# Three fp32r terms for the spatial unit's two projections, and parameter operations behind the first modulation

## What is computed

```python
z = jax.nn.gelu(hn @ c_w_in[j], approximate=False)     # 1024 -> 2048
u, vv = jnp.split(z, 2, axis=-1)
vv = layer_norm_2(vv, c_ln_g[j], c_ln_b[j])
h = h + spatial_gating(u, vv, c_w_s[j], c_b_s[j]) @ c_w_out[j]
h = h + moe_swiglu(rms_norm_2(h, ln_ffn[i]), ...)      # top 2 of 8 experts
```

## Time and profile before

| | us |
|---|---|
| median of 3 runs | 2120.82 (2120.63 to 2123.67) |
| the profiled execution | 2116.54 |
| its span, first to last instruction | 2114.8 |
| TensorE busy | 2023.5 (96%) |
| DVE busy | 1354.8 (64%) |
| ACT busy | 923.1 (44%) |

### The profile page before, as it was taken

The page is one execution under the profiler, slowest core; times in us unless marked ns, Lnnn a source line. Parts: engine busy times, 40 slices in busy tenths (PEclk is TensorE's granted clock), DMA queues, the critical chain, the costliest instruction groups (busy, mean ns, idle before and its releaser), DMA issues. The chain is left out here.

```text
span 2114.8 us, 28776 instructions
## 1 busy us (share of the span) xinstructions
PE 2023.5 (96%) x12095; PEld 1805.3 (85%) x12095; DVE 1354.8 (64%) x1671; ACT 923.1 (44%) x1066; POOL 71.5 (3%) x109
## 2 busy tenths in 40 slices
PE   4998999999999999999999989999999999999998
PEld 3876888787878877899998889999999999898976
DVE  6687897352464134666532269787878787878862
ACT  2511111212125102343432357676767676666654
POOL 2000000000000010100120000000000000000000
PEclk8998999999999999999999999999999999999999
DMA  9745221335143242255763259898989999899980
GB/s 319 262 122 172 66 81 61 120 135 185 40 159 119 81 161 100 63 191 186 192 233 133 83 199 367 313 356 323 356 322 335 346 330 346 328 352 331 348 316 21
DMA packets 225852, 452.22 MB, mean 214 GB/s; under 512 B 6944, under 2 KB 91176, under 8 KB 225720
## 3 DMA queue, kind: packets, MB, share of 16 engines
q1 hardware_dynamic: 222400, 445.44, 60.1%
q0 software_dynamic: 1632, 4.75, 0.8%
q10 hardware_dynamic: 1688, 0.15, 0.1%
HBM read 448.21 MB, written 2.10 MB: 213 GB/s over the span
## 5 line engine op out<-in xcount | busy, mean ns | idle before, releaser
L1752 DVE TENSOR_TENSOR ring_r<-ring,his_r 128x2816 fp32r<-128x2816 f32 (+1 forms) x192 | 587.1, 3086 | 59.8 <-ACT his_r L1360 59.6
L1360 ACT ACTIVATE his_r<-ring 128x2816 fp32r<-128x2816 f32 (+1 forms) x192 | 491.2, 2561 | 198.0 <-DMA ring<-in_moe_w_dram 184.6
L1046 PE MATMUL bank<-his_r,hg_r 128*128 128x352 f32 x2048 | 355.5, 325 | 0.8 <-ACT hg_r L1382 0.8
L1046 PEld LDWEIGHTS bank<-his_r,hg_r 128*128 128x128 f32 x2048 | 332.9, 188 | 2.0 <-issue 0.9
L2220 PE MATMUL bank<-hT,ring 128*128 128x256 f32 x912 | 218.0, 396 | 3.2 <-ACT hT L2542 1.8
L2220 PEld LDWEIGHTS bank<-hT,ring 128*128 128x128 f32 x912 | 177.4, 198 | 32.5 <-issue 7.0
L1046 PE MATMUL bank<-ring_r,hg_r 128*128 128x352 f32 x1024 | 186.1, 324 | 0.0
L2002 PE MATMUL bank<-arena,ring 128*128 128x256 f32 x800 | 178.2, 380 | 1.8 <-ACT cw L1302 0.7
L2002 PEld LDWEIGHTS bank<-arena,ring 128*128 128x128 f32 x800 | 151.3, 190 | 24.4 <-issue 1.3
L1046 PEld LDWEIGHTS bank<-ring_r,hg_r 128*128 128x128 f32 x1024 | 169.2, 188 | 0.0
L2002 PE MATMUL bank<-hT,ring 128*128 128x256 f32 x624 | 142.9, 387 | 5.0 <-ACT hT L2542 3.4
(11 more groups left out here) (495 smaller groups left out, 2529.7 us busy)
## 6 DMA issues: line engine op xcount, KB each, us to landing
ring<-in_moe_w_dram SPq DMA_DIRECT2D x128, 1408.0 KB, 8.3
ring<-in_moe_w_dram SPq DMA_DIRECT2D x48, 1536.0 KB, 8.8
ring<-in_even_w_in_dram SPq DMA_DIRECT2D x28, 1024.0 KB, 6.0
ring<-in_ffn_w_dram SPq DMA_DIRECT2D x22, 1024.0 KB, 5.4
ring<-in_ada_w_dram SPq DMA_DIRECT2D x20, 1024.0 KB, 9.4
ring<-in_odd_w_in_dram SPq DMA_DIRECT2D x9, 2048.0 KB, 7.7
ring<-in_moe_w_dram SPq DMA_DIRECT2D x16, 1024.0 KB, 6.5
ring<-in_a_w_in_dram SPq DMA_DIRECT2D x6, 2048.0 KB, 7.9
```

Of the source, the lines that this page charges most:

```text
L1046: ins = mm(bank[first + m][:, 0:WC], x[:, KT // 2 * late + k, :], w[:, k, WC * m:WC * m + WC], start=(not late and k == 0 and s == "hg_hi" ...
L1360: A(moe_hi(n), moe_w(n), ACT.Copy).then_inc(sem("moe_hi"), 1)
L1752: V.tensor_tensor(moe_lo(n), moe_w(n), moe_hi(n).bitcast(F32), ALU.subtract).then_inc(sem("moe_lo"), 1)
```

## The change

Tiles of `cin` and `cout` are computed in three fp32r terms. H2 becomes a pair: h2_r[0], the rounded value written by ACT, and h2_r[1], the remainder, by DVE (`rest`). CU gets its rounded copy from ACT and its remainder from DVE (`cu_lo`), a quarter at a time. The weights are split in 12 units u of two tiles: ACT casts (`c_cast`) into one of three buffers, DVE writes the remainder into the ring (`c_lo`). Casts 0 to 2 and remainders 0, 1 lie beside `pg0`, the others beside `cin` and `cout`. The heads (`c_first`) take hi and lo for both tiles over k, then the remainder of x. Second, three operations on AUX at the start of the kernel, with the wait for the parameters, are moved behind ada(3, 0) and the wait for the first norm.

```diff
--- before.py
+++ after.py
@@ -127,6 +127,9 @@
         fa_hi_r = sb_r("fa_hi_r", 12288, FT, T)
         fa_lo_r = sb_r("fa_lo_r", 17920, FT, T)
         f2_r = [sb_r(f"f2_r{n}", off, FT, P) for n, off in enumerate((25088, 0, 2816))]
+        cb_r = [sb_r(f"cb_r{n}", off, KT, T)[:, :, :] for n, off in enumerate((2048, 15360, 25088))]
+        h2_r = [sb_r("h2_hi_r", 13312, KT, T)[:, :, :], sb_r("h2_lo_r", 19456, KT, T)[:, :, :]]
+        cu_r = [sb_r("cu_hi_r", 21504, KT, T)[:, :, :], sb_r("cu_lo_r", 4096, KT, T)[:, :, :]]
         at_lo_r = sb_r("at_lo_r", 9984, FT, SLOTS)
         arena = sb("arena", [P, ARENA])
 
@@ -498,6 +501,22 @@
 
             return ffn_r[:, phases["f13"]["place"][j]["slot"]].rearrange("p (k n) -> p k n", k=KT)
 
+        C_HI = [cb_r[u % 3] for u in range(8)] + [cb_r[2 * (u % 2)] for u in range(4)]
+        C_FREE = {3: 0, 4: 1, 5: 2, 6: 3, 7: 4, 8: 6, 9: 5, 10: 8, 11: 9}
+
+        def c_half(u, flat=ring_flat):
+
+            name, v = ("cin", u) if u < 8 else ("cout", u - 8)
+            return view(phases[name], v // 2, flat)[:, :, T * (v % 2):T * (v % 2) + T]
+
+        def hi_made(u):
+
+            return u + 1 if u < 10 else u + 5
+
+        def c_done(u):
+
+            return phases["cin"]["t0"] + 2 * u + 2
+
         BCH_AT = [0, 2, 3, 5, 6, 8, 9, 11, 12]
         CONV_AT = {3: (0,), 4: (1,), 5: (2,), 6: (3,)}
         CGATE_AT = {7: (0, 1), 8: (2, 3)}
@@ -955,7 +974,45 @@
                     spatial_turn(2)
                     spatial_turn(3)
 
-            pe_gemm("cin", lambda k: H2[:, k, :], [], ready=xg_waits(5), lead=2, mid=lambda: norm_rest(5), prev="pg0", between=beside_cin)
+            def c_terms(q, x, bk, after):
+
+                u, m = q // 2, q % 2
+                hi, lo = C_HI[u], c_half(u, ring_r_flat)
+                for w, y in ((hi, x[0]), (hi, x[1]), (lo, x[0])):
+                    if w is lo:
+                        pe.wait_ge(sem("c_lo"), u + 1)
+                    for k in range(KT):
+                        ins = mm(bk[:, 0:T], w[:, k, m * P:m * P + P], y[:, k, :], start=(w is hi and y is x[0] and k == 0),
+                                 stop=(w is lo and k == KT - 1))
+                ins.then_inc(acc_ready, 1)
+                after(q % 16)
+
+            def c_first(u, x, ready, mid, last):
+
+                hi, lo = C_HI[u], c_half(u, ring_r_flat)
+                pe.wait_ge(sem("c_hi"), u + 1)
+                pe.wait_ge(sem("c_lo"), u + 1)
+                for k in range(KT):
+                    pe.wait_ge(*ready(k))
+                    for w in (hi, lo):
+                        for m in range(2):
+                            mm(bank[m][:, 0:T], w[:, k, m * P:m * P + P], x[0][:, k, :], start=(k == 0 and w is hi), stop=False)
+                mid()
+                for m in range(2):
+                    for k in range(KT):
+                        pe.wait_ge(*last(k))
+                        ins = mm(bank[m][:, 0:T], hi[:, k, m * P:m * P + P], x[1][:, k, :], start=False, stop=(k == KT - 1))
+                    ins.then_inc(acc_ready, 1)
+
+            for q in range(2):
+                pe.wait_ge(*took("pg0", 5 + q))
+            c_first(0, h2_r, xg_waits(5), lambda: norm_rest(5), lambda k: (sem("c_rest"), k + 1))
+            beside_cin(0)
+            beside_cin(1)
+            for q in range(2, 16):
+                pe.wait_ge(*(took("pg0", 5 + q) if q < 4 else took("cin", q - 3)))
+                pe.wait_ge(sem("c_hi"), q // 2 + 1)
+                c_terms(q, h2_r, bank[q % 4], beside_cin)
             pe.wait_ge(sem("toks_taken"), TK_V + 4)
             pe.wait_ge(sem("pool_made"), MADE["spatial"])
             for g in range(8):
@@ -987,8 +1044,13 @@
                     route(q - 4)
 
             pe.wait_ge(*took("cin", 16))
-            pe_gemm("cout", lambda k: CU[:, k, :], [], ready=lambda k: (sem("spatial_taken"), k // 2 + 1), lead=2, banks=2,
-                    parts=(range(0, 2), range(2, 4), range(4, 6), range(6, 8)), between=beside_cout)
+            c_first(8, cu_r, lambda k: (sem("c_hi"), 10 + k // 2 + 1), lambda: None, lambda k: (sem("c_rest"), KT + k // 2 + 1))
+            beside_cout(0)
+            beside_cout(1)
+            for q in range(2, 8):
+                pe.wait_ge(*took("cout", q - 1))
+                pe.wait_ge(sem("c_hi"), hi_made(8 + q // 2))
+                c_terms(16 + q, cu_r, bank[q % 2], beside_cout)
             norm_rest(6, 4)
             for ct in range(4, KT):
                 route(ct)
@@ -1316,12 +1378,21 @@
                 act.wait_ge(*took(f"pg{i}", q + 1))
                 A(PG[:, q, :], PG[:, q, :], ACT.Sigmoid).then_inc(sem("activated"), 1)
 
+            def c_cast(u):
+                name, v = ("cin", u) if u < 8 else ("cout", u - 8)
+                wait_chunk(act, name, v // 2, 0)
+                if u in C_FREE:
+                    act.wait_ge(acc_ready, c_done(C_FREE[u]))
+                A(C_HI[u], c_half(u), ACT.Copy).then_inc(sem("c_hi"), 1)
+
             for q in range(KT + 1):
+                if q in (1, 3, 5):
+                    c_cast(q // 2)
                 if q < KT:
                     gate(0, q)
                 if q >= 1:
                     act.wait_ge(sem("embedded"), q)
-                    A(H2[:, q - 1, :], xT[:, q - 1, :], ACT.Identity, scale=col("mix1", q - 1)).then_inc(sem("xg_ready"), 1)
+                    A(h2_r[0][:, q - 1, :], xT[:, q - 1, :], ACT.Identity, scale=col("mix1", q - 1)).then_inc(sem("xg_ready"), 1)
                     square(5, q - 1)
             root(5)
             def spatial_taken(b):
@@ -1332,6 +1403,11 @@
                 act.wait_ge(*took("cin", q + 1))
                 v = CU[:, q - KT, :] if q >= KT else CVV[:, q, :]
                 A(v, v, ACT.Gelu).then_inc(sem("activated"), 1)
+                if q % 2 == 1 and q < 10:
+                    c_cast(q // 2 + 3)
+                elif q == 13:
+                    c_cast(8)
+                    c_cast(9)
                 if q == 2:
                     for b in range(2):
                         act.wait_ge(sem("toks_ready"), TK_W + b + 1)
@@ -1351,6 +1427,9 @@
                     spatial_taken(1)
             spatial_taken(2)
             spatial_taken(3)
+            for b in range(4):
+                act.wait_ge(sem("spatial_taken"), b + 1)
+                A(cu_r[0][:, 2 * b:2 * b + 2, :], CU[:, 2 * b:2 * b + 2, :], ACT.Copy).then_inc(sem("c_hi"), 1)
 
             def hi(n):
 
@@ -1364,6 +1443,8 @@
                     hi(0)
                     hi(1)
                 act.wait_ge(*took("cout", q + 1))
+                if q in (1, 3):
+                    c_cast(10 + q // 2)
                 A(hT[:, q, :], xT[:, q, :], ACT.Identity, scale=col("ffn1", q)).then_inc(sem("xg_ready"), 1)
                 square(6, q)
             root(6)
@@ -1699,6 +1780,10 @@
                 step(V.tensor_tensor(FX[:, q % 2, :], bank[q % 4][:, 0:T], nr[:, :], ALU.mult))
                 V.tensor_tensor(xT[:, q, :], FX[:, q % 2, :], xT[:, q, :], ALU.add).then_inc(acc_taken["dve"], 1)
 
+            def c_lo(u):
+                dve.wait_ge(sem("c_hi"), hi_made(u))
+                V.tensor_tensor(c_half(u, ring_r_flat), c_half(u), C_HI[u].bitcast(F32), ALU.subtract).then_inc(sem("c_lo"), 1)
+
             def ple(i, nrm):
 
                 dve.wait_ge(sem("norm_rooted"), nrm + 1)
@@ -1706,14 +1791,30 @@
                 if i:
                     dve.wait_ge(*took("pp1", 8))
 
+                def rest(q):
+                    if i == 0:
+                        dve.wait_ge(sem("xg_ready"), KT * XN[5] + q + 1)
+                        V.scalar_tensor_tensor(h2_r[1][:, q, :], xT[:, q, :], col("mix1", q), h2_r[0][:, q, :].bitcast(F32), ALU.mult, ALU.subtract)\
+                            .then_inc(sem("c_rest"), 1)
+
                 def add(q):
                     dve.wait_ge(sem("activated"), (KT + 16) * i + q + 1)
                     step(V.tensor_tensor(PG[:, q, :], PG[:, q, :], (PP, PP1)[i][:, q, :], ALU.mult))
                     V.tensor_tensor(xT[:, q, :], xT[:, q, :], PG[:, q, :], ALU.add).then_inc(sem("embedded"), 1)
 
+                def beside(q):
+                    if q >= 1:
+                        add(q - 1)
+                    if q >= 2:
+                        rest(q - 2)
+                    if i == 0 and q in (3, 6):
+                        c_lo(q // 3 - 1)
+
                 take_gemm(dve, f"pg{i}", lambda q, lin, b: V.tensor_tensor(PG[:, q, :], b, RPG, ALU.mult), banks=(4, 2)[i],
-                          between=lambda q: add(q - 1) if q else None)
+                          between=beside)
                 add(KT - 1)
+                rest(KT - 2)
+                rest(KT - 1)
 
             ple(0, 4)
 
@@ -1721,6 +1822,10 @@
             step(V.reciprocal(RIN, nr[:, :]))
 
             def beside_cin(q):
+                if q % 2 == 0 and q < 12:
+                    c_lo(q // 2 + 2)
+                elif q >= 14:
+                    c_lo(q - 6)
```

(18 more changed lines are left out.)

## The result

| | median us | lowest to highest | profiled execution | its span |
|---|---|---|---|---|
| before | 2122.16 | 2120.63 to 2123.67 | 2116.54 | 2114.8 |
| after | 2110.84 | 2108.59 to 2111.79 | 2110.74 | 2109.0 |

After stands to before as 0.9943, with a 95% interval of 0.993 to 0.9956; of 2122 us that is 12.1 less, between 9.3 and 14.9. The medians themselves differ by 11.3. The forecast was -9.3 and 2111.5 us.

The account below looks back on a forecast made before the run. TensorE, almost without idle time, was taken as the bound in the projections and experts. Tiles -11.8, hand-over losses 0.1, 0.05, 1.25 and 1.2 gave -9.2; with -0.1 for the parameter operations, -9.3 from 2120.8: 2111.5 us, range 2106 to 2117.

Parts of the forecast that it names:

- The tile: In `cin` and `cout`, a tile of 24 matmuls takes 2.86 us, 0.59 less; 11.8 us over the 20 tiles outside the heads.
- Head of `cin`: Start of `cin`: c_lo(1) on DVE delays an eviction; TensorE idle 0.6 and 0.7 us; head gives back its 1.2 and 0.1.
- Layer norm and v: Tile 12 to the spatial matmuls: casts 8 and 9 on ACT delay the copies; 1.1 us gained of 2.36, 1.25 lost.
- Head of `cout`: After the spatial matmuls start: TensorE waits for CU's last two quarters; the head's own gain goes and 1.2 us more.
- The cover: Steady part of `cin`: per two tiles ACT and DVE need about 3.1 us, against TensorE's 2 x (2.86 + 0.43): covered.
- The squares: Layer norm's squares in `cin`: with cast 7 and remainder 7 around them, ACT arrives just when tile 10 ends; 0.05 us lost.
- Routing chain: Between `cout` and the experts: left as it is by the change and moved earlier as a block.
- that rival: Experts bound by the weight stream: their end does not move and the time stays at 2120.8 us; chance 0.06.
- the rival that ended slower: Gaps before the spatial matmuls and in `cout`'s head lower the clock for tiles 2 to 7: +4.3, 2125.1 us; chance 0.06.
- Parameter operations: At the kernel's start: moved, ada(2, 0) still waits for TensorE's group 0 sum; -0.1 us, between 0.1 more and 0.3 less.
- First z matmul: Behind the start's modulation: a shift of its start by more than 0.5 us would show the forecast wrong.
- The reference of the sum: Whole kernel: -9.3 us taken from the median of 2120.8, giving 2111.5; 2107.2 for an execution like the profiled one.

Follow-up runs that it names:

- The mended kernel: Changed kernel with cast 9 moved behind the layer norm's root on ACT and CU's four remainders behind all four products on DVE: 2109.42 us, ratio 0.9941.
- two kernels with a shifted balance: Changed kernel with an added DVE pass ahead of each of 12 weight remainders: 2128.94 us; changed kernel without the third term in 20 tiles: 2102.95 us.
- the kernel with the third accumulator: Changed kernel with a separate accumulator for column group 2, so ada(2, 0) doesn't wait for TensorE's sum of group 0: 2108.08 us, ratio 0.9933.

## Why the forecast held, step by step

From pg0 to the experts, by the distances of the two TensorE timelines:

| stretch | before | after | difference | forecast |
|---|---|---|---|---|
| pg0 to the end of pg0 | 28.05 | 27.87 | -0.18 | 0 |
| head of `cin`, to tile 2 | 8.22 | 8.49 | +0.27 | +0.1 |
| tiles 2 to 11 | 41.44 | 35.34 | -6.10 | -5.85 |
| tile 12 to the spatial matmuls | 16.79 | 15.26 | -1.53 | -1.1 |
| spatial matmuls to tile 2 of `cout` | 10.58 | 11.59 | +1.01 | +1.2 |
| tile 2 to the end of `cout` | 26.12 | 22.50 | -3.62 | -3.54 |
| routing chain | 20.73 | 21.34 | +0.61 | 0 |
| sum | | | -9.54 | -9.2 |

Outside the routing chain these distances repeat to 0.02 us in the other profiles with the same stage, two of the old one and three of the new. Without that chain the change is worth 10.15 us, 0.95 more than forecast, most of it in the tiles and before the spatial matmuls.

- **The tile.** 2.86 us forecast, 2.85 measured; 3.29 with the sum, 3.28 measured. The rule of the Trainium skill ("TensorE: Matmul & The Clock Gate", Part 3, The mechanism) by which such loads would stand bare isn't borne out: by the estimate from it a tile took some 5.4 us.
- **Head of `cin`.** Both waits came, from the releasers named: 0.23 (0.6 forecast) and 0.66 (0.7).
- **Layer norm and v.** Two waits, 0.83 and 0.69; tile 12 to the spatial matmuls 15.26 where I had 15.7. The mended kernel shows that cast 9 made the first of them, 0.69 us of the distance.
- **Head of `cout`.** Two waits of 0.72, both on ACT's casts; S + 11.59 where I had S + 11.75. The mended kernel shows that the order of DVE's remainders cost 1.15 of it.
- **The cover.** It held in the outcome, but the forecast's reason was short. It set 3.1 us on ACT and 3.1 on DVE side by side against 6.58, as if 3.5 were free; they stand in series, a round takes 4.92, and 1.64 are free.
- **The squares.** 0.05 us was right here. The two kernels with a shifted balance lost 5.80 and 4.06 us at exactly this place.
- **Routing chain.** The 0.61 us are not the change's: the gathering matmuls take 5.74 us in the profile of before, 6.34 in that of after, and 6.40 and 6.37 in the two other kernels that have the old stage.
- **Experts.** The distance to the end is 873.8 before and 873.7 after: nothing of the gain is lost to the weight stream, so that rival is out.
- **The clock.** 1.00 through both heads, so the rival that ended slower didn't happen. That its mechanism exists is seen in the two kernels with waits of 4 to 6 us. The Trainium skill ("TensorE: Matmul & The Clock Gate", Part 1) says that the array is throttled by default and that activity releases it; the traces agree, with 3.78 us for 8 sums behind the longest wait and 1.89 for the next 8, one tile later in the same kernel.
- **Parameter operations.** Releaser and mechanism as forecast, the sign was not: -0.1 forecast, with at most 0.1 more as the bad end; +0.19 measured. The slip is in the forecast's own sum. With the stall ending at 25.5 instead of 25.37 and the 0.23 us paid later on the same engine, what stands behind comes 0.13 us later and not 0.1 earlier.
- **First z matmul.** I had called a shift of over 0.5 us a sign of an error. It came, 2.5 us: 2.32 up to the sum for column group 0, by the late rise of the clock, and 0.19 by the move. What failed is the bound itself: I took it from one execution of before, and the start of the kernel has two forms.
- **The reference of the sum.** The stage and the move together say -9.4 against the profile of before and -10.0 against the two others with the old stage; the medians say -11.3, and the half without the move says 2111.08 at a ratio of 0.9954, or -9.8. The 1.3 to 1.9 us between lie within the interval, and well within what the untouched code scatters (below). That 2111.5 came within 0.7 us of 2110.84 is in part luck: the difference was forecast 2.0 us too small and the reference 1.3 too low.

## What to carry to other kernels

Sum up such a change by distances between named instructions, one hand-over at a time, and put each distance beside the same one in a second execution; here the stage said -9.5 to -10.2 us in the four pairs of a kernel with the change in it and one without, while their whole spans said anything from -5.8 to -15.8. When an engine is given less to do, add up the round that the helping engines make in series, and not the load of each: what the tiles take beyond that round is the slack of the loop (1.64 us here, where the loads alone said 3.5). Then list the places where the engine waits for another and look for what stands just ahead of them: there the losses come due. A wait that is taken away shows the next one; before counting on its length, ask who else releases the instruction behind it, here a shared accumulator and then the weights.

## What the runs showed of the hardware

- fp32r matmuls of 128x128 weights and 256 columns follow each other at 119 ns with a new weight load for each, both of FFN and of these projections (2.85 us for 24).
- The clock falls with waits of this size: behind 5.80 us idle the stretch has 0.77 on the mean, and 8 fp32 matmuls of 256 columns take 3.78 us instead of 1.89. After the waits of 0.7 to 0.8 us in both heads it stayed at 1.00.
- At the start of the kernel the same 16 sums take 3.62 us in some executions and 4.7 to 5.5 in others, in both forms of the kernel; the clock rises late in the slow ones. 40 idle matmuls ahead bring a first rise at 7.6 to 9.0 us and make the turns of x quicker (1.97 us for 3.67); the upper level outlasted the next wait of 2.69 and 2.77 us, fell at 21.2 in one execution, and held until 29.5 in the other. In a third, with a wait of 4.33 us, it fell at 21.7, within the wait.
- Between the first z matmul and pg0 the same code takes 1041.9 to 1050.7 us in the profiles of this study. It is the clock: of the two ends, by stretch (columns as in the earlier trace rows), the kernel with the third accumulator (1041.9) had

```profile
45.00:300.00 255.00, 235.78 (x1685) 199.35 (x1684) 208.25 (x406) 61.99 (x125) 10.85 (x17) 0.97 0.49 152
```

and the one with the mended hand-overs (1050.4)

```profile
45.00:300.00 255.00, 236.08 (x1654) 199.41 (x1655) 203.16 (x394) 61.99 (x127) 10.86 (x17) 0.95 0.47 148
```

  From 600 to 900 us the clock is 0.99 in the first and 0.98 in the second; the other stretches agree. 0.02 of 255 us and 0.01 of 300 are 8.1 of the 8.5 us, within the rounding of the clock. In all thirteen profiles this distance, less what the trace's clock records say was lost to the lower level (20.9 to 31.6 us), is 1018.0 to 1021.0 us. What makes the clock differ is open.
